# A hybrid encoder layer with 32 experts: TensorE's middle pairs written as a loop, a weight ring of 16 slots in place of 17, and four small moves around it

## The reference, cut to what matters

```
logits = (x2d @ w_router) + b_router
top_logits, top_idx = lax.top_k(logits, TOP_K)            # 4 of 32
gates = softmax(top_logits)
...
gu = xe @ w_gu[e] + b_gu[e]                               # xe: the rows routed to expert e
g, u = minimum(gu[:, :FF], 7), clip(gu[:, FF:], -7, 7)
h = (u + 1) * (g * sigmoid(1.702 * g))
y = h @ w_down[e] + b_down[e]                             # weighted by the gates and added to the rows
```

## Time and profile before

| | us |
|---|---|
| median of 3 runs | 1093.73 |
| lowest and highest | 1093.47, 1096.12 |
| the profiled execution | 1092.89 |
| its span, first to last instruction | 1090.8 |

### The profile page before, as it was taken

The page is one execution under the profiler, slowest core; times in us unless marked ns, Lnnn a source line. Parts: engine busy times, 40 slices in busy tenths (PEclk is TensorE's granted clock), DMA queues, the critical chain, the costliest instruction groups (busy, mean ns, idle before and its releaser), DMA issues.

```text
span 1090.8 us, 11590 instructions
## 1 busy us (share of the span) xinstructions
PE 1030.3 (94%) x5061; PEld 491.0 (45%) x5062; DVE 316.8 (29%) x489; ACT 97.0 (9%) x164; POOL 7.8 (1%) x19
## 2 busy tenths in 40 slices
PE   8999999999999999989899999999898989899886
PEld 6767454444444443434343344344343535353333
DVE  3533121322323232312323132323232232323133
ACT  3222130100000000000000010100000000001011
POOL 1100000000000000000000000000000000000000
PEclk9999999999999999999999999999999999999999
DMA  9940769999999999999999999999999999999994
GB/s 348 326 98 2 231 242 383 415 430 427 425 428 409 427 427 427 426 428 426 428 429 425 428 429 426 428 425 428 427 427 427 428 426 427 427 427 420 421 421 176
DMA packets 58931, 420.66 MB, mean 386 GB/s; under 512 B 23092, under 2 KB 23392, under 8 KB 29568
## 3 DMA queue, kind: packets, MB, share of 16 engines
q1 hardware_dynamic: 55776, 418.53, 93.3%
q10 hardware_dynamic: 2800, 0.95, 0.3%
q0 software_dynamic: 304, 0.41, 0.1%
HBM read 418.29 MB, written 1.58 MB: 385 GB/s over the span
## 4 chain that ended last, share of the span: by engine, by line
PE 62%; DMA 36%; DVE 1%; issue 0%; ACT 0%; DVEq 0%
PE ps L779 31%; DMA ring<-in_w_gu_dram 30%; PE ps L718 6%; PE ps L794 6%; DMA ring<-in_w_down_dram 6%; PE ps L641 5%; PE ps L820 3%; PE ps L659 3%; PE ps L534 2%; PE ps L805 1%; PE ps L781 1%; PE ps L670 1%; PE ps L903 1%; PE ps L544 1%; PE ps L610 0%; PE ps L823 0%
## 5 line engine op out<-in xcount | busy, mean ns | idle before, releaser
L779 PE MATMUL ps<-ring,xT 128*64 128x512 f32 x1024 | 465.1, 607 | 35.0 <-DMA ring<-in_w_gu_dram 34.2
L781 PE MATMUL ps<-ring,xT 128*64 128x512 f32 x1024 | 465.7, 608 | 0.0
L779 PEld LDWEIGHTS ps<-ring,xT 128*64 128x64 f32 x1024 | 137.4, 139 | 313.2 <-issue 308.2
L794 PE MATMUL ps<-ring,he 128*64 128x512 f32 x480 | 213.7, 595 | 10.0 <-DMA ring<-in_w_down_dram 9.6
L796 PE MATMUL ps<-ring,he 128*64 128x512 f32 x480 | 214.2, 596 | 0.0
L1506 DVE TENSOR_TENSOR x<-ps,x 128x512 f32<-128x512 f32 (+1 forms) x84 | 54.3, 683 | 299.0 <-PE ps L820 271.1
L781 PEld LDWEIGHTS ps<-ring,xT 128*64 128x64 f32 x1024 | 137.3, 139 | 0.0
L794 PEld LDWEIGHTS ps<-ring,he 128*64 128x64 f32 x480 | 62.9, 137 | 141.2 <-issue 141.1
L718 PEld LDWEIGHTS ps<-oh,hn 128*128 128x128 f32 x768 | 95.5, 196 | 11.7 <-issue 9.2
L718 PE MATMUL ps<-oh,hn 128*128 128x128 f32 x768 | 98.2, 283 | 0.0
L1138 ACT COPY gu_sb<-ps 128x1024 f32<-128x1024 f32 x16 | 16.2, 1012 | 592.1 <-PE ps L781 592.1
(11 more groups left out here) (207 smaller groups left out, 589.9 us busy)
## 6 DMA issues: line engine op xcount, KB each, us to landing
ring<-in_w_gu_dram SPq DMA_DIRECT2D x103, 2048.0 KB, 29.4
ring<-in_w_down_dram SPq DMA_DIRECT2D x50, 2048.0 KB, 30.4
ring<-in_w_gu_dram SPq DMA_DIRECT2D x50, 1024.0 KB, 25.4
ring<-in_w_down_dram SPq DMA_DIRECT2D x26, 1024.0 KB, 28.2
w_chc<-in_w_in_dram SPq DMA_DIRECT2D x1, 4096.0 KB, 21.9
w_qkv<-in_w_in_dram SPq DMA_DIRECT2D x4, 768.0 KB, 9.4
w_b<-in_w_in_dram SPq DMA_DIRECT2D x1, 2048.0 KB, 28.5
w_o<-in_w_out_dram SPq DMA_DIRECT2D x2, 1024.0 KB, 28.1
```

Source lines behind the costliest of these rows:

```text
L779: even = mm(gu_banks(j)[0:CAP, n, :], xT[j % 2][:, k, 0:CAP], ring[:, first % RING, cols], start=(k == 0), stop=(k == KT - 1))
L781: odd = mm(gu_banks(j)[CAP:P, n, :], xT[j % 2][:, k, CAP:P], ring[:, second % RING, cols], start=(k == 0), stop=(k == KT - 1))
L794: even = mm(out[0:CAP, half, :], hid[:, f, 0:CAP], ring[:, first % RING, cols], start=(f == 0), stop=(f == FT - 1))
```

## The change

- RING is 16. The SBUF region keeps the size of 17 slots.
- TensorE's loop over pairs becomes a function `pair(j)`: pairs 0, 1, 14 and 15 are called as before, pairs 2 to 13 are a hardware loop of six passes with two pairs in its body. Waits in the body compare with 15 registers that are set before the loop and raised at the end of each pass. 48 chunks per pass are three times the ring, so that slots are the same in each pass.
- The marks of pair 1 are made in `ohg` ahead of finishing the routing, so that its gather can begin behind step 0 of pair 0. Its PSUM banks change from 4 and 5 to 6 and 7, those of the turned gates from 7 to 4. The products behind steps 0 to 6 of pair 0 are now 5, 5, 6, 5, 4 (and the turned gates), 5 and 4.
- BIASED is 12 in place of 6. `b_dn` is loaded by GpSimd in one transfer once the counts are known, in place of ScalarE's four at j == 3.
- `turn_oh(PAIRS)` moves from behind step 0 of the last pair's down steps to behind step 2 of the down steps ahead of them.
- The result leaves in three transfers: SP the left halves of both prompt tiles, ACT both right halves, SP the sample rows.

```diff
-    RING = 17
+    RING = 16
-        ring_region = Region("ring_region", RING * SLOT)
+        ring_region = Region("ring_region", (RING + 1) * SLOT)
...
-            first = 4 if j < 2 else 2
+            first = (4, 6, 2)[min(j, 2)]
-        GT = ps[0:NE, 7, 0:NT * P]
+        GT = ps[0:NE, 4, 0:NT * P]
-        BIASED = 6
+        BIASED = 12
...
-            sp.wait_ge(right_out[0], 1)
-            sp.dma_start(out_rows[:, 0, HALF:D], x[:, 0, HALF:D]).then_inc(y_stored, 16)
+            sp.wait_ge(left_out[0], 1)
+            sp.wait_ge(left_out[1], 1)
+            sp.dma_start(out_rows[:, :, 0:HALF], x[:, 0:2, 0:HALF]).then_inc(y_stored, 16)
...
+            pool.wait_ge(counts_ready, 2)
+            pool.dma_start(b_dn[:, :], b_down[0]).then_inc(b_down_in, 16)
...
+            def landed(j, e, c):
+                told, value = LANDED[NTH[(e, c)]]
+                pe.wait_ge(told, so_far(j, value, PER_LOOP // RING * 16))
+            IN_LOOP, PER_LOOP = range(2, PAIRS - 2), 2 * 2 * CH
...
+            GROWING = ([(value, 2) for value in range(1, 6)] + [(value, 2 * 2 * NT) for value in range(2, 2 * 2 * NT + 1, 2)]
+                       + [(16 * turn, PER_LOOP // RING * 16) for turn in range(3, 7)])
...
+            def so_far(j, value, step):
+                if j not in IN_LOOP:
+                    return value
+                if (value, step) not in growing:
+                    growing[value, step] = pe.alloc_register(f"so_far_{value}_{step}")
+                return growing[value, step]
...
+                            pe.wait_ge(oh_ready, 2)
+                            gather(1, 0, some=slice(0, 1))
...
+                    if j == PAIRS - 1 and m == 2:
+                        pe.wait_ge(ohT_ready, PAIRS - 1)
+                        turn_oh(PAIRS)
...
+            pair(0)
+            pair(1)
+            for value, step in GROWING:
+                pe.reg_mov(so_far(IN_LOOP[0], value, step), value)
+            with pe.Fori(0, len(IN_LOOP) // 2):
+                for j in IN_LOOP[:2]:
+                    pair(j)
+                for value, step in GROWING:
+                    pe.reg_add(growing[value, step], growing[value, step], step)
+            for j in (PAIRS - 2, PAIRS - 1):
+                pair(j)
...
-                if m == 0:
-                    pe.wait_ge(ohT_ready, L)
-                    turn_oh(PAIRS)
-                else:
+                if m > 0:
...
-                if j == 3:
-                    for q in range(NE // 8):
-                        act.dma_start(b_dn[8 * q:8 * q + 8, :], b_down[0, 8 * q:8 * q + 8, :]).then_inc(b_down_in, 16)
...
-            act.wait_ge(left_out[0], 1)
-            act.wait_ge(left_out[1], 1)
-            act.dma_start(out_rows[:, :, 0:HALF], x[:, 0:2, 0:HALF]).then_inc(y_stored, 16)
+            act.wait_ge(right_out[0], 1)
             act.wait_ge(right_out[1], 1)
-            act.dma_start(out_rows[:, 1, HALF:D], x[:, 1, HALF:D]).then_inc(y_stored, 16)
+            act.dma_start(out_rows[:, :, HALF:D], x[:, 0:2, HALF:D]).then_inc(y_stored, 16)
...
             move_xT(0, slice(0, 2)).then_inc(xT_first, 1)
+            mark(2, to=ohg).then_inc(oh_ready, 1)
...
-                if j + 1 < PAIRS:
+                if 1 <= j < PAIRS - 1:
                     dve.wait_ge(gathered, 2 * (j + 1))
                     mark(2 * j + 2).then_inc(oh_ready, 1)
```

More of the change, by code:

```diff
@@ L715, in gather @@
                 out = gathered_banks(j)
+                marks = ohg if j == 1 else oh
                 for k in range(half * KT // 2, (half + 1) * KT // 2)[some]:
@@ L771, in turn_gates @@
                 last.then_inc(gates_turned, 1)
+            def landed(j, e, c):
+                told, value = LANDED[NTH[(e, c)]]
+                pe.wait_ge(told, so_far(j, value, PER_LOOP // RING * 16))
             def gate_up(j, k):
                 first, second = NTH[(2 * j, k)], NTH[(2 * j + 1, k)]
-                for n in (first, second):
-                    pe.wait_ge(*LANDED[n])
+                landed(j, 2 * j, k)
+                landed(j, 2 * j + 1, k)
                 for n in range(FLAT // 512):
@@ L787, in down @@
                 first, second = NTH[(2 * j, GUC + m)], NTH[(2 * j + 1, GUC + m)]
-                for n in (first, second):
-                    pe.wait_ge(*LANDED[n])
+                landed(j + 1, 2 * j, GUC + m)
+                landed(j + 1, 2 * j + 1, GUC + m)
                 for a in range(FPC):
@@ L825, in scatter, with pair @@
                 last.then_inc(scattered, 1)
-            for j in range(PAIRS):
-                pe.wait_ge(*((xT_front, j + 1) if j else (xT_first, 1)))
+            IN_LOOP, PER_LOOP = range(2, PAIRS - 2), 2 * 2 * CH
+            assert PER_LOOP % RING == 0
+            for j in IN_LOOP[2:]:
+                for e in (2 * j - 4, 2 * j - 3):
+                    for at, c in [(e, c) for c in range(GUC)] + [(e - 2, c) for c in range(GUC, CH)]:
+                        a, b = NTH[(at, c)], NTH[(at + 4, c)]
+                        assert b == a + PER_LOOP and LANDED[b] == (LANDED[a][0], LANDED[a][1] + PER_LOOP // RING * 16)
+            GROWING = ([(value, 2) for value in range(1, 6)] + [(value, 2 * 2 * NT) for value in range(2, 2 * 2 * NT + 1, 2)]
+                       + [(16 * turn, PER_LOOP // RING * 16) for turn in range(3, 7)])
+            growing = {}
+            def so_far(j, value, step):
[4 more added lines that the diff above has]
+                return growing[value, step]
+            def pair(j):
+                if j == 0:
+                    pe.wait_ge(xT_first, 1)
+                else:
+                    pe.wait_ge(xT_front, so_far(j, j + 1, 2))
                 if j == 1:
@@ L844, in _ @@
                             gather(0, 0, (1,), some=slice(2, 4)).then_inc(gathered, 1)
+                            pe.wait_ge(oh_ready, 2)
+                            gather(1, 0, some=slice(0, 1))
                         if k == 1:
                             gather(0, 1, (1,), some=slice(0, 2)).then_inc(first_gathered, 1)
+                            gather(1, 0, some=slice(1, 2))
                         if k == 2:
@@ L894, in _ @@
                         else:
-                            pe.wait_ge(added, 2 * NT * (j - 1))
-                        turn_oh(j)
+                            pe.wait_ge(added, so_far(j, 2 * NT * (j - 1), 2 * 2 * NT))
+                        turn_oh(so_far(j, j, 2))
+            pair(0)
[7 more added lines that the diff above has]
+                    pe.reg_add(growing[value, step], growing[value, step], step)
+                assert set(growing) == set(GROWING)
+            for j in (PAIRS - 2, PAIRS - 1):
+                pair(j)
             L = PAIRS - 1
```

55 lines of the change are left out of this document (29 added, 26 removed).

## The result

The changed kernel takes 1088.61 us (median of 6 runs, 1086.03 to 1090.66) beside 1093.81 us of the kernel before (6 runs): a ratio of 0.9943, 95% interval 0.9932 to 0.9955. That is 6.2 us faster by the ratio and 5.2 by the medians. The forecast was 1088.7 us, faster. Its profiled execution took 1089.28 us with a span of 1087.1.

What follows compares the result with a forecast made beforehand. The prediction took the weight transfers, not TensorE, to bound the kernel. Its terms summed to -5.0 us from the profiled 1092.89, giving 1087.9 profiled and a median of 1088.7 us; range 1086.5 to 1095 for 8 times in 10.

Steps and rivals of the forecast that it cites:

- What bounds the kernel: From about 200 us, weight transfers at 421 to 428 GB/s set the pace; TensorE has some 4 us margin a pair.
- 1, the fetches: TensorE's loop body stays in instruction memory, sparing 23 fetches carried by eight DMA engines: -3.6 us.
- the unkept body: Rival: each jump of TensorE's loop fetches anew, +1.2 us in place of -3.6, 1093.5 us; chance 0.30.
- 2 to 4, the front: Ring of 16 slots, pair 1's marks and gathers, moved `b_dn`: double loads -0.6, front +0.9, hole at 340 us -1.2 us.
- a backlog of one more chunk fills those holes: In the stretches after 165 us, one more waiting chunk fills the stream's holes: about 2.8 us back.
- the ring of 16: One slot less: -0.6 us from nine more double loads, 2.5 us lost at the front, about 2.8 us back.
- `b_dn`: Moving its load to pair 0 removes the hole at 340 us, -1.2 us, with 0.5 us coming back at the front.
- The marks: Reordered marks and gathers of pair 1 delay loads waiting for steps of pair 0: +0.7 us net.
- 5, 6, 7: Bias products moved to pair 14, register waits with additions and jumps, and last marks: each 0 us, covered by waits.
- The rival at 1101 us: TensorE becomes the bound through the loop body's 468 register waits, at 0.10 us each on the path; chance 0.11.
- 8, three transfers: At the end, the result's left halves go out earlier and ACT's held-up second issue disappears: -0.5 us, bounds -1.2 and +0.3.
- The sum: All terms, -3.6 - 0.6 + 0.9 - 1.2 - 0.5, give -5.0 us against the profiled execution of 1092.89 us.

Runs made afterwards that it cites:

- E1: Changed kernel with its twelve middle pairs written out instead of looped, waits on constants: 1093.05 us, ratio 0.9995 to the kernel before.
- E11: Changed kernel again, unaltered, on the same chip as E10: 1087.87 us, ratio 0.9949 to the kernel before.
- E9: Changed kernel with only pairs 2 to 7 in the loop (three passes), pairs 8 to 15 written out: 1091.03 us, ratio 0.9969 to the kernel before.
- E2: Changed kernel with the passes written out, register waits and additions kept, no jump: 1092.52 us, ratio 0.9987 to the kernel before.
- E3: Changed kernel with three passes of four pairs in place of six of two: 1093.68 us, ratio 0.9999 to the kernel before.
- E6: Kernel before with a ring of 16 slots and nothing else: 1093.99 us, ratio 0.9993 to the kernel before.
- E8: Changed kernel with the old order of marks, gathers and PSUM banks in pair 0: 1087.14 us, ratio 0.9934 to the kernel before.
- E10: Changed kernel with the old order in pair 0 and the first 40 chunks loaded singly: 1087.22 us, ratio 0.9940 to the kernel before.
- E5: Kernel before with the result in three transfers and nothing else: 1095.26 us, ratio 1.0007 to the kernel before.
- E12: E1 without TensorE's branch to further rounds, the rounds behind it and the count load it tests: 1091.81 us, ratio 0.9978 to the kernel before.
- E4: Changed kernel with its first 40 chunks loaded singly in place of 24: 1088.56 us, ratio 0.9953 to the kernel before.

## Why the prediction was right

**What bounds the kernel** held: 42.4 us of waits for the ring, 428 GB/s in every window of the loop. Nothing that TensorE had to do more was seen in the time.

**1, the fetches.** Predicted about 20 packets and -3.6 us in the stream (bounds -1.8 and a loss); measured 20 and -4.0 (E1 against the change and E11, with the dose of E9 between). The mechanism was right and the eight engines too, which the prediction chose from the end of the stream and which the landings of E1 and E2 show. The packet was sized too low: it takes 1.06 us itself but holds its engine up by 1.5, and so costs the end 0.18 us and not 1.25 / 8 = 0.16. Twenty-two packets less at 0.18 are the 4.0. That a packet delays the one engine that carries it, and that a chunk lands with its slowest part, is borne out by the straight line, by the landings of the parts, and by the end of the stream. Before, the rate went from 422 to 221 and 209 GB/s and held there; after, at the same distance from the last waits:

```profile
1069.00:1070.00 1.00, 1.00 (x6) 0.65 (x4) 0.21 (x1) 0.00 (x0) 0.00 (x0) 1.00 1.06 391
...
1071.00:1072.00 1.00, 1.00 (x8) 0.37 (x6) 0.68 (x2) 0.00 (x0) 0.00 (x0) 1.00 0.85 320
1072.00:1073.00 1.00, 1.00 (x8) 0.35 (x6) 0.00 (x0) 0.00 (x0) 0.00 (x0) 1.00 0.65 252
1073.00:1074.00 1.00, 1.00 (x5) 0.27 (x2) 0.00 (x0) 0.00 (x0) 0.00 (x0) 1.00 0.31 119
```

The fall begins later and is steep: by the landings of the sixteen parts of a chunk the engines are 3.7 us apart at the end, 7.7 before. The chance of 0.30 for the unkept body stands as a fair one: only E3, with 45 packets, tells that it was a matter of size.

**2 to 4, the front.** Predicted +0.9 - 0.6 - 1.2 = -0.9 us; in the stream 0.0 (E1). The step that failed is "a backlog of one more chunk fills those holes". It filled those of 180 to 200 us and opened new ones behind them, of 1.0 to 1.2 us at 230 us, so the ring of 16 came out at +0.4 in the stream of one profile (E6) where -0.6 + 2.5 - 2.8 = -0.9 was worked out; the timed runs (0.9993, 0.9982 to 1.0003) can't tell the two apart. `b_dn` was sized at -0.7 net. Its window came back whole, and alone it measured -2.0 us (-3.0 to -1.0), at -0.1 in the stream of its profile. The interval lies beyond the term, and the reason stays open. The marks, predicted at +0.7, are 0.0 in the stream, and up to 1 us by E8 and E10, unresolved.

**5, 6, 7.** Nothing, as predicted. The products at L831 ran from 953.5 us with 4.4 us of idle time left in their window. E2 bounds the register waits: 1092.52 us against 1093.05 without them, and TensorE no less idle. The rival at 1101 us needed 0.084 us a wait and is out.

**8, three transfers.** Predicted -0.5 (bounds -1.2 and +0.3) from the issues. The stretch to the last issue is 17.85 us before and after, as the prediction had it; the landing is 2.3 us shorter. By E1's profile 0.8 of that is the three transfers, the other 1.5 are the fetch at the end, which the prediction did not have; the changed kernel is spared it, as the straight programs of E5 and E6 are too. Timed alone the three transfers show nothing (E5, 1.0007, 0.9994 to 1.0019).

**The sum** was -5.0 us against the profiled execution; by the ratios of its two measurements, 0.9943 and 0.9949, the change brings 6.2 and 5.6. The loop brings 5.4 by E1's 0.9995 against their mean, 4.0 in the stream and about 1.5 in the landing. What the sum had too much at the front (0.9), and too little in the fetches (0.4) and at the end (1.8), made up for each other in part. That the median came out within 0.1 us of the forecast is luck: the two measurements of the change alone lie 0.7 us apart. The windows of two pairs were to take 116.7 us and took 117.4: they are cut where TensorE begins a pair and not where a chunk lands, so they can't show what one pass gains.

## What to carry to other kernels

When the transfers set the pace, as here at 428 GB/s, the program itself is a transfer: here each packet of TensorE's code that isn't fetched again is worth 0.18 us. The loop paid because its body wasn't fetched again from pass to pass: one of about 1190 instructions wasn't (20 packets, 42 without the loop), one of twice that was (45). So ask of a loop first whether the queue of the instructions shrinks in the page; where it didn't (E3), the loop was worth nothing. Read such a gain as the stretch between two events on the bound engine, since here whole spans of one kernel differ by more than the parts in question, and look at what is fetched behind the last instruction.

## What the runs showed of the hardware that was not expected

**The clock.** In the profiled execution of the change TensorE's granted clock fell from 1.00 to 0.50 of full speed in step 0 of pair 0, from 159.2 to 162.6 us:

```profile
157.22 0.74 PE L722 MATMUL ps<-oh,hn 128*128 128x128 f32 x4
158.54 0.64 PE L787 MATMUL ps<-ring,xT 128*64 128x512 f32 x1 [0.59 <-DVE xT L1502]
...
160.51 1.06 PE L787 MATMUL ps<-ring,xT 128*64 128x512 f32 x1
...
161.37 1.06 PE L787 MATMUL ps<-ring,xT 128*64 128x512 f32 x1
162.22 0.81 PE L787 MATMUL ps<-ring,xT 128*64 128x512 f32 x1
```

Pairs of products start 0.85 us apart there, 0.43 otherwise, and step 0 takes 5.28 us in place of 3.6. The same kernel on another execution, E11, kept the clock, with the same 0.59 us of idle time before the step:

```profile
155.27 0.74 PE L722 MATMUL ps<-oh,hn 128*128 128x128 f32 x4
156.60 0.64 PE L787 MATMUL ps<-ring,xT 128*64 128x512 f32 x1 [0.59 <-DVE xT L1502]
...
158.37 0.59 PE L787 MATMUL ps<-ring,xT 128*64 128x512 f32 x1
158.79 0.59 PE L787 MATMUL ps<-ring,xT 128*64 128x512 f32 x1
```

Of the fourteen profiles five have the fall (the change, E2, E9, E10 and E12), with and without the loop, with the new order of pair 0 and with the old; E11 and E8 are without it under either order. So neither decides it, and the same kernel has it in one execution and not in the other. It is 1.7 us that the stream never makes up, because its loads wait for that very step: the stream behind it is 901.15 us long with the fall and 901.23 without. Inside the stream the clock falls too, after waits for chunks (in the kernel before to 0.50 from 414.4 us on, for 3.4 us, behind 2.69 us of waiting), but there the transfers cover it: two pairs take 117.4 to 117.6 us whether the window's mean is 1.00 or 0.97. Together with the start of step 0, which lies between 156.4 and 159.2 us, it makes one kernel's executions differ by over 3 us: E11's span is 1083.7 us, that of the first profile of the same kernel 1087.1.

**The end.** A fetch of code that is never executed held the landing of the result up by 1.6 us (E1 against E12), where it met the engine that carried the last part.

**The fetches.** A packet of 1.06 us made its engine 1.5 us late in the full stream, and eight of the sixteen engines carried such packets in turn. So the engines drifted apart by 7.7 us in 900, and the stream ended with the late eight.

**The front.** A hole of 1.2 us in the stream was closed (E4) and came up again ahead of it, so the stream was not shorter: 901.59 us against 901.15 and 901.23.
